# Up-projections with 512 moving columns that hold a low and a high part, and convolution taps split between ScalarE and VectorE

## The reference, cut to what matters

```
def swiglu(h, w_gate, w_up, w_down):                      # feed-forwards 0 to 3
    return (jax.nn.silu(h @ w_gate) * (h @ w_up)) @ w_down

def conv_ffn(h, w_up, cw, cb, w_down):                    # feed-forwards 4 and 5
    gu = causal_dwconv(h @ w_up, cw, cb)                  # 3 taps over tokens, by channel
    g, u = jnp.split(gu, 2, axis=-1)
    return (jax.nn.gelu(g, approximate=True) * u) @ w_down
```

## Time and profile before

| | |
|---|---|
| median of three runs | 1931.16 us (1926.08 to 1932.69) |
| the profiled execution | 1931.93 us, span 1930.3 us |
| TensorE busy | 1819.3 us, 94% of the span |
| VectorE busy | 1420.4 us, 74% |
| ScalarE busy | 940.5 us, 49% |
| GpSimd busy | 128.5 us, 7% |
| up-projection matmuls | 3 x 2112 of 256 columns |

### The profile page before, as it was taken

How to read it: one execution, slowest core, us unless ns; L and a number is a source line. 1 busy time by engine, 2 the same in 40 slices (tenths; PEclk the granted TensorE clock), 3 DMA queues, 4 the chain that set the end, 5 groups by cost and what they waited for, 6 DMA issues and landing times.

```text
span 1930.3 us, 31852 instructions
## 1 busy us (share of the span) xinstructions
PE 1819.3 (94%) x11710; PEld 1620.2 (84%) x11710; DVE 1420.4 (74%) x2280; ACT 940.5 (49%) x1360; POOL 128.5 (7%) x168
## 2 busy tenths in 40 slices
PE   2999999889999999999999999999889999979998
PEld 2999777789988997788878799987679987769996
DVE  6778798687778778877665565548869866877894
ACT  3444465454435443555454454445764445664443
POOL 0001010000010000000000000000011100001110
PEclk8999999899999999999999999999999999999999
DMA  9878765457787778454540165545144554324553
GB/s 383 289 277 294 269 230 197 140 186 271 276 306 271 276 267 282 170 175 175 191 155 1 48 233 184 185 175 207 66 177 176 187 185 164 117 88 164 185 180 125
DMA packets 63267, 382.62 MB, mean 198 GB/s; under 512 B 7088, under 2 KB 7088, under 8 KB 26688
## 3 DMA queue, kind: packets, MB, share of 16 engines
q1 hardware_dynamic: 42624, 300.96, 43.3%
q0 software_dynamic: 19984, 77.93, 11.2%
q10 hardware_dynamic: 576, 2.60, 0.3%
HBM read 380.42 MB, written 1.05 MB: 198 GB/s over the span
## 4 chain that ended last, share of the span: by engine, by line
PE 86%; DVE 8%; ACT 4%; issue 2%; DMA 1%; SPq 0%; DVEq 0%; ACTq 0%
PE ps L496 13%; PE ps L497 13%; PE ps L498 13%; PE ps L463 11%; PE ps L465 11%; PE ps L464 11%; DVE ring_lo L1461 1%; PE ps L764 1%; PE ps L517 1%; PE ps L519 1%; PE ps L518 1%; PE ps L790 1%; PE ps L777 1%; PE ps L544 1%; DMA arena<-in_mod 1%
## 5 line engine op out<-in xcount | busy, mean ns | idle before, releaser
L1461 DVE TENSOR_TENSOR ring_lo<-ring,w_hi 128x1024 fp32r<-128x1024 f32 x534 | 647.7, 1222 | 341.4 <-ACT w_hi L1051 336.7
L1051 ACT ACTIVATE w_hi<-ring 128x1024 fp32r<-128x1024 f32 x556 | 584.2, 1057 | 601.2 <-PE ps L498 307.6
L496 PE MATMUL ps<-h_lo,w_hi 128*128 128x256 f32 x2112 | 602.3, 285 | 13.0 <-DVE ring_lo L1461 11.4
L497 PE MATMUL ps<-h_hi,w_hi 128*128 128x256 f32 x2112 | 601.3, 285 | 0.0
L498 PE MATMUL ps<-h_hi,ring_lo 128*128 128x256 f32 x2112 | 600.9, 285 | 0.0
L496 PEld LDWEIGHTS ps<-h_lo,w_hi 128*128 128x128 f32 x2112 | 409.4, 194 | 14.5 <-DVE ring_lo L1461 11.6
L497 PEld LDWEIGHTS ps<-h_hi,w_hi 128*128 128x128 f32 x2112 | 409.5, 194 | 0.0
L498 PEld LDWEIGHTS ps<-h_hi,ring_lo 128*128 128x128 f32 x2112 | 409.2, 194 | 0.0
L463 PE MATMUL ps<-w_hi,h_lo 128*128 128x512 f32 x604 | 246.2, 408 | 13.8 <-DVE h_lo L1873 6.4
L464 PE MATMUL ps<-ring_lo,h_hi 128*128 128x512 f32 x604 | 238.9, 396 | 0.0
L465 PE MATMUL ps<-w_hi,h_hi 128*128 128x512 f32 x604 | 238.7, 395 | 0.0
(11 more groups left out here) (322 smaller groups left out, 1888.9 us busy)
## 6 DMA issues: line engine op xcount, KB each, us to landing
ring<-in_stream SPq DMA_DIRECT2D x278, 1024.0 KB, 4.8
arena<-in_mod POOLq DMA_DIRECT2D x128, 512.0 KB, 5.6
arena<-in_mod SPq DMA_DIRECT2D x14, 512.0 KB, 15.6
gate<-in_wide POOLq DMA_DIRECT2D x3, 1536.0 KB, 10.0
arena<-in_nsaw POOLq DMA_DIRECT2D x2, 1072.0 KB, 9.2
arena<-in_konst POOLq DMA_DIRECT2D x1, 1295.5 KB, 9.5
arena<-in_mixw POOLq DMA_DIRECT2D x2, 576.0 KB, 10.6
x<-in_x ACTq DMA_DIRECT2D x1, 1024.0 KB, 12.7
```

Source lines behind the costliest of these rows:

```text
L496: nc.tensor.matmul(dst, hi, x_lo, start=(r == 0 and i == 0 and b % 2 == 0), stop=False)
L497: nc.tensor.matmul(dst, hi, x_hi, start=False, stop=False)
L1051: nc.scalar.activation(w_hi[:, q % SPLITS, :], ring[:, half % SLOTS, (q % 2) * QUARTER:(q % 2 + 1) * QUARTER], ACT.Copy).then_inc(w_hi_rea ...
L1461: v.tensor_tensor(ring_lo[:, slot, cs], ring[:, slot, cs], w_hi[:, q % SPLITS, :], ALU.subtract).then_inc(w_lo_ready, 1)
```

## The change

The low and high part of `h` now lie beside each other (`h_both`), and a new `up_wide` multiplies the high weights by both at once, 512 columns into one bank: the left half collects high by low, the right half high by high, and a second matmul of 256 columns adds low by high to the right half. A step uses four banks (`WIDE_BANKS`), so all eight serve two steps. In feed-forwards 0 to 3 step 0 keeps the former form.

Whoever empties a step adds the halves: ScalarE copies the left halves of two banks at a time into `wa`, VectorE adds the right halves. Silu and the product then read `wa`. In feed-forwards 4 and 5 ScalarE also computes the newest tap with its bias from `wa` into `wb`, and VectorE accumulates the two others from `wa`; the order of splits, taps and gelu is changed on both engines. TensorE waits there for the added halves (`conv_whole`) and no longer for the taps. The norms in front of these two use the banks in another order, and the gate matmuls wait for the last step's product, since they share banks 6 and 7 with it.

```diff
+WIDE_BANKS = ((0, 1, 6, 7), (2, 3, 4, 5))
...
-        h_lo = over("h_lo", slab_at["hT"], [P, KC, T], F32R)
-        h_hi = over("h_hi", slab_at["h_hi"], [P, KC, T], F32R)
+        h_both = over("h_both", slab_at["hT"], [P, 2, KC, T], F32R)
+        h_lo, h_hi = h_both[:, 0, :, :], h_both[:, 1, :, :]
...
-            first = (4, 5, 6, 7, 2, 3) if m in (2, 5) else (2, 3, 6, 7, 4, 5)
+            first = (4, 5, 6, 7, 2, 3) if m in (2, 5) else (6, 7, 2, 3, 4, 5) if m in (7, 9) else (2, 3, 6, 7, 4, 5)
...
+            def up_wide(q, banks, it, per, fresh=None):
+                for r in range(4):
+                    low_part(q + r, it, per)
+                    slot, half, buf = ((q + r) // 2) % SLOTS, ((q + r) % 2) * QUARTER, (q + r) % SPLITS
+                    for i in range(2):
+                        if fresh is not None:
+                            pe.wait_ge(norm_lo, fresh + 2 * r + i + 1)
+                        for b in range(4):
+                            if fresh is not None and (r, i, b) == (0, 0, 3):
+                                pe.wait_ge(norm_lo, fresh + 2)
+                            o = i * 512 + b * P
+                            hi, lo = w_hi[:, buf, o:o + P], ring_lo[:, slot, half + o:half + o + P]
+                            nc.tensor.matmul(ps[:, banks[b], :].rearrange("p (w t) -> p w t", w=2), hi, h_both[:, :, 2 * r + i, :],
+                                             start=(r == 0 and i == 0), stop=False)
+                            mm = nc.tensor.matmul(ps[:, banks[b], T:2 * T], lo, h_hi[:, 2 * r + i, :], start=False, stop=(r == 3 and i == 1))
+                    mm.then_inc(quarter_done, 1)
...
+                    if conv:
+                        if v0 + j >= RING or it is not None:
+                            pe.wait_ge(conv_whole, val(it, 2 * (v0 + j - RING + 1), 2 * RING))
+                        up_wide(q0 + 4 * j, WIDE_BANKS[j % 2], it, TURNQ, 8 * m if j == 0 else None)
+                        return
...
                     if f < 3 and kk in GATES[f]:
+                        pe.wait_ge(h_ready, UPS * (f + 1))
                         gates(*GATES[f][kk])
```

ScalarE, feed-forwards 0 to 3, steps 1 to 10:

```diff
+                    for n, b in enumerate(WIDE_BANKS[j % 2][::2]):
+                        low = ps[:, b:b + 2, 0:T]
+                        nc.scalar.activation(wa[:, n * 512:(n + 1) * 512].rearrange("p (b t) -> p b t", b=2), low, ACT.Copy).then_inc(low_kept, 1)
+                    keep_hi(f, j - 1, it)
+                    act.wait_ge(gate_whole, val(it, (UPS - 1) * f + j))
+                    nc.scalar.activation(wa[:, 0:512], wa[:, 0:512], ACT.Silu).then_inc(silu_ready, 1)
```

ScalarE, feed-forwards 4 and 5 (`keep_low` is the two copies, `taps` is Identity with scale and bias on 256 columns, twice a call):

```diff
                 def step(j, it):
                     q = q0 + 4 * j + 4
+                    if j > 0:
+                        keep_low(j - 1, it)
                     split(q, q + 2, it, TURNQ)
                     if j > 0:
+                        taps(j - 1, it, 0)
+                        taps(j - 1, it, 1)
+                    split(q + 2, q + 3, it, TURNQ)
+                    if j > 0:
                         gelu(j - 1, it)
-                    split(q + 2, q + 4, it, TURNQ)
+                    split(q + 3, q + 4, it, TURNQ)
```

VectorE, feed-forwards 0 to 3 (the addition runs twice a step):

```diff
+                        ins = v.tensor_tensor(low, ps[:, b:b + 2, T:2 * T], low, ALU.add)
+                    keep(j - 1, it)
+                    v.tensor_tensor(wb[:, half:half + 512], wa[:, 512:1024], wa[:, 0:512], ALU.mult).then_inc(h_ready, 1)
```

VectorE, feed-forwards 4 and 5 (`whole` waits for a copy and adds the right halves, 512 columns, twice a call):

```diff
-                        tick.mark(v.tensor_scalar(acc[:, c, :], src(c, 0), w, bias, ALU.mult, ALU.add))
-                            ins = v.scalar_tensor_tensor(out=acc[:, c, lag:T], in0=src(c, lag), scalar=w, in1=acc[:, c, lag:T],
+                            ins = v.scalar_tensor_tensor(out=acc[:, c, lag:T], in0=wa[:, c * T:(c + 1) * T - lag], scalar=w, in1=acc[:, c, lag:T],
...
-                    split(q, q + 1, it, TURNQ)
+                    if j > 0:
+                        whole(j - 1, it)
+                    split(q, q + 2, it, TURNQ)
                     if j > 0:
                         conv(j - 1, it, (0, 1))
-                    split(q + 1, q + 2, it, TURNQ)
-                    if j > 0:
                         conv(j - 1, it, (2, 3))
                     split(q + 2, q + 3, it, TURNQ)
```

More of the change, by code:

```diff
@@ L1140, in ffn_conv, with keep_low, taps @@
             def ffn_conv(f):
-                q0, v0 = BASE[f"ffn{f}"], UPS * (f - 4)
+                q0, v0, l = BASE[f"ffn{f}"], UPS * (f - 4), f - 4
+                def keep_low(j, it):
+                    act.wait_ge(quarter_done, val(it, q0 + 4 * j + 4, TURNQ))
+                    if v0 + j > 0 or it is not None:
+                        act.wait_ge(fconv_ready, val(it, v0 + j))
+                    for n, b in enumerate(WIDE_BANKS[j % 2][::2]):
+                        nc.scalar.activation(wa[:, n * 512:(n + 1) * 512].rearrange("p (b t) -> p b t", b=2), ps[:, b:b + 2, 0:T],
+                                             ACT.Copy).then_inc(conv_low, 1)
+                def taps(j, it, n):
+                    y = v0 + j
+                    act.wait_ge(conv_whole, val(it, 2 * y + n + 1, 2 * RING))
+                    if y > 0 or it is not None:
+                        if n == 0:
+                            act.wait_ge(gelu_ready, val(it, y))
+                        else:
+                            act.wait_ge(hid_ready_all, val(it, UPS * f + j))
+                    for c in (2 * n, 2 * n + 1):
+                        o = n * FC + c % 2 + 2 * j
+                        w = cols[:, bass.ds(val(it, COLS["fc_w"] + (l * 3 + 2) * 44 + o, 2 * RING), 1)]
+                        bias = cols[:, bass.ds(val(it, COLS["fc_b"] + l * 44 + o, 2 * RING), 1)]
+                        ins = nc.scalar.activation(wb[:, c * T:(c + 1) * T], wa[:, c * T:(c + 1) * T], ACT.Identity, bias=bias, scale=w)
+                    ins.then_inc(conv_tap, 1)
                 def gelu(j, it):
@@ L1159, in ffn_conv @@
                         step(PEEL + r, it)
+                keep_low(UPS - 1, None)
+                taps(UPS - 1, None, 0)
+                taps(UPS - 1, None, 1)
                 gelu(UPS - 1, None)
@@ L1629, in step @@
                                 mod_turn(t, it, MOD_UP * (j - peel) + r // 2)
+                    half = (j % 2) * 512
+                    if j == 0:
+                        dve.wait_ge(silu_ready, u + 1)
+                        v.tensor_tensor(wb[:, half:half + 512], ps[:, b + 1, :], wa[:, 0:512], ALU.mult).then_inc(h_ready, 1)
+                        return
+                    for n, b in enumerate(WIDE_BANKS[j % 2][::2]):
+                        dve.wait_ge(low_kept, val(it, 2 * ((UPS - 1) * f + j - 1) + n + 1, 2 * turn))
+                        low = wa[:, n * 512:(n + 1) * 512].rearrange("p (b t) -> p b t", b=2)
+                        ins = v.tensor_tensor(low, ps[:, b:b + 2, T:2 * T], low, ALU.add)
+                        if n == 0:
+                            ins.then_inc(gate_whole, 1)
+                        else:
+                            tick.mark(ins)
+                    keep(j - 1, it)
                     dve.wait_ge(silu_ready, val(it, u + 1, turn))
[L1631 to L1634, removed]
+                    tick.settle()
+                    v.tensor_tensor(wb[:, half:half + 512], wa[:, 512:1024], wa[:, 0:512], ALU.mult).then_inc(h_ready, 1)
                 for j in range(peel):
@@ L1671, in ffn_conv, with whole @@
                 acc = wb[:, :].rearrange("p (c t) -> p c t", c=4)
-                def conv(j, it, pair):
[L1675 to L1683, removed]
-                        tick.mark(v.tensor_scalar(acc[:, c, :], src(c, 0), w, bias, ALU.mult, ALU.add))
+                def whole(j, it):
+                    for n, b in enumerate(WIDE_BANKS[j % 2][::2]):
+                        dve.wait_ge(conv_low, val(it, 2 * (v0 + j) + n + 1, 2 * RING))
+                        y = wa[:, n * 512:(n + 1) * 512].rearrange("p (b t) -> p b t", b=2)
+                        v.tensor_tensor(y, ps[:, b:b + 2, T:2 * T], y, ALU.add).then_inc(conv_whole, 1)
+                def conv(j, it, pair):
+                    dve.wait_ge(conv_tap, val(it, 2 * (v0 + j) + pair[0] // 2 + 1, 2 * RING))
                     for lag in (1, 2):
@@ L1733, in ffn_conv @@
                 d0 = q0 + UPQ
+                whole(UPS - 1, None)
                 conv(UPS - 1, None, (0, 1))
```

27 lines of the change are left out of this document (18 added, 9 removed).

## The result

The changed kernel took **1919.41 us** (median of 4 runs, 1917.54 to 1920.25) against 1931.93 for the kernel before (median of 4 on the same chip): ratio 0.9938, 95% interval 0.9915 to 0.9962. It is faster, by 12.5 us; 26.2 were forecast, and 1919.41 lies 0.4 above the range. The profiled execution took 1920.25.

The account below looks back on a forecast made before the run. TensorE, busy 94% of the span, was taken to bound the kernel. From 1931.93 us, 26.4 saved by matmuls and 0.2 lost at the turns gave 1905.7 us; own range 1901 to 1909, full range 1900 to 1919.

Parts of the forecast that it names:

- The matmuls: Up-projections: one fixed 13.3 ns saved per triple, 32 triples a step, 62 steps, 26.4 us in all.
- 226.7 + 120.0 = 346.7 ns: Up-projection triple after the change: one matmul of 512 columns and one of 256, against 360.0 ns before.
- the two pieces of the operand: Wide matmul's moving operand, two 256-column pieces 8 KB apart: 226.7 ns if like contiguous columns, 240 if nothing is saved.
- The turn to the down-projection: Convolution feed-forwards: splits behind copies, taps and gelu are only just ready for TensorE; 0.2 us lost in all.
- I take 0.1 us per feed-forward: Loss at the tight turn to the down-projection in each of the two convolution feed-forwards.
- The first rival: GpSimd and VectorE exclude each other, served in turn; turn loses 2.3 + 0.3 us per convolution feed-forward; 1910 to 1918; chance 0.27.
- nothing in this trace speaks for or against blocking: GpSimd's splits beside taps: those taps all read PSUM, so the trace cannot show whether two-SBUF-input VectorE work excludes GpSimd.
- GpSimd kept out: Rival: GpSimd gets no turn in VectorE's unbroken rows, 3.7 us lost every second convolution step; 1942 to 1943; chance 0.12.
- Evictions in the first four: Feed-forwards 0 to 3: added copies and additions on ScalarE and VectorE are covered by TensorE; cost 0.
- banks of the norms: Two norms using the banks in another order, with the wait for a second chunk before the fourth bank: cost 0.
- the number of matmuls gone: Up-projections: 62 steps x 32 = 1984 matmuls and as many weight loads gone.
- no steady step of the up-projections waits: Up-projection steps: eviction and split work is ready before TensorE needs it, so TensorE has no waits there.

Follow-up runs that it names:

- experiment 1: Changed kernel with low and high part of each chunk side by side in memory, so the 512 moving columns are one run: 1917.30 us.
- experiment 5: Changed kernel with GpSimd making no low parts; VectorE makes them in the convolution's feed-forwards: 1915.49 us.
- experiment 6: Changed kernel with the additions written back into PSUM and the taps reading there, banks held until the taps are done: 1917.42 us.
- experiment 4: Changed kernel with the splits of down quarters 4 and 5 moved ahead of the last step's taps on ScalarE and VectorE: 1913.74 us.
- experiment 3: Changed kernel with each wide matmul undone into two of 256 columns in the same bank, all else kept: 1936.59 us.
- experiment 12: Changed kernel with the splits-before-taps turn, plus four wide then four narrow matmuls opening each feed-forward's first wide step only: 1905.15 us.

## Why the prediction was wrong

**The matmuls: the direction right, the term mis-sized.** The step that failed is "226.7 + 120.0 = 346.7 ns", a sum of two spacings read from rows of one width each. In turn the two widths take 346.7 or 353.3 per triple, and the changed kernel showed 353.3 in all six feed-forwards: 13.2 us instead of 26.4. The prediction bounded the unknown by the two pieces of the operand; experiment 1 shows that these were not it. Its upper bound, 360, did hold the value, but its own range, 1901 to 1909, took in only the low end, and no rival had a value between the two. What was left out is that a mix of widths is itself a thing that the trace of before doesn't show. By the formula of the Trainium skill (TensorE: Matmul & The Clock Gate, section Back-to-back issue gap), which that section gives for an isolated matmul, 2.5 ns per triple would have gone, 5.0 us as an estimate; 6.7 ns and 13.2 us went here, so the measurement decides.

**The turn to the down-projection: 4.9 us instead of 0.2.** The step that failed is "I take 0.1 us per feed-forward". It rested on VectorE idle time, 1.4 us of a step, that the exclusion took away (VectorE is busy 11.28 of 11.31). The first rival had this right: 2.3 + 0.3 was forecast under it, 2.45 measured. Without GpSimd (experiment 5) and with one operand of the taps in PSUM (experiment 6) 2.2 to 2.4 us come back at each turn, which shows the cause; the order (experiment 4) is the remedy. The sentence "nothing in this trace speaks for or against blocking" was true, and 0.27 was too little for this rival; its own range, 1910 to 1918, still misses, by the matmuls.

**GpSimd kept out** did not come: its longest split in feed-forward 4 lasted 3.47 us, in the fourth step, and from then on 2.40 to 2.42.

**Evictions in the first four, banks of the norms: cost 0** held (experiment 3). A step of feed-forward 3's kind, without modulation, has room to spare: 82.9 of 124.7 us of VectorE, 68.3 of ScalarE.

```profile
1107.77:1232.43 124.66, 124.66 (x736) 109.70 (x737) 82.87 (x96) 68.26 (x88) 0.00 (x0) 1.00 0.56 201
```

**The rest of the sum.** 13.2 gained and 4.9 lost make 8.3, while the span is 11.7 shorter. The prediction saw little to win from the clock and has no term for it; the other 3.4 are the net of stages whose granted clock differed. The up-projection of feed-forward 3 got 4.1 us shorter, about half of it by its first 14 us (before, then after):

```profile
1114.83:1128.83 14.00, 14.00 (x100) 14.00 (x101) 11.79 (x19) 8.24 (x11) 0.00 (x0) 0.84 0.75 302
1107.77:1121.77 14.00, 14.00 (x110) 13.68 (x111) 13.02 (x21) 9.81 (x13) 0.00 (x0) 1.00 0.81 304
```

The attention behind feed-forward 0 took 160.81 us instead of 163.39, at 0.94 instead of 0.93. Against that, the up-projection of feed-forward 1 got only 0.6 shorter where 2.1 were due, at 0.98 instead of 1.00. No part of the change aimed at that, and stages of other runs show either, so these 3.4 us are luck; that the clock is behind all of them is read from these rows and was not tested.

**What was seen right:** the number of matmuls gone, ScalarE's copies (two in 1.09) and first taps (four in 2.08, 2.0 forecast), VectorE's additions (1.28 for two) and taps (3.23 for eight), and that no steady step of the up-projections waits.

## What to carry to other kernels

A spacing read from a row of equal instructions holds for that row; when a change mixes kinds, give the mix bounds of its own, and look at several stages of the result before believing one number. Before moving an operand from PSUM to SBUF on VectorE, see what GpSimd reads at that moment; if it must read SBUF, put work with one SBUF input beside it, or drop GpSimd's help. At the end of a pipelined loop, keep the loop's order of splits before taps: what the next stage needs first should not stand behind the last step's leftovers.

## What was unexpected of the hardware

Wide (512) and narrow (256) matmuls in turn, each with its own weights, ran in one of two steady rhythms, 346.7 or 353.3 ns per pair at a granted clock of 1.00, each kept over a whole feed-forward of ten steps where nothing stalled them. Equal matmuls showed one mean spacing only (120.0, 226.7), though once, in experiment 12, in a cycle of 117 to 124. Four and four took 351, pairs and eights 349. As far as the runs show, which rhythm came was carried over from what ran before, could be shifted by four wide and four narrow ones or by a short stall, and differed between two feed-forwards of one execution. Each trace shows one execution, so the rhythms of the others are not known. What in the engine keeps this phase was not found.
